# A fourth projection unit beside each head pair's RWKV preparation, two instead of three dealt out over the pair's groups

## What is computed

```python
h = rmsnorm(x, norm_g) * (1 + scale) + shift
proj = h @ w_in      # split into r, k, v, wd, ad, g, gq, gk, gv, ..., qd, kvd, kpe, ...
...
def step(s, inp):                       # per head, forward and backward in time
    sa = einsum('bhij,bhj->bhi', s, -kk_t)
    s = s * w_t + sa[..., None] * (kk_t * a_t) + v_t[..., None] * k_t
    return s, einsum('bhij,bhj->bhi', s, r_t)
...
o = groupnorm(outs[0] + outs[1]) + bonus
y_a = (o * silu(rw_g)) @ rw_out
```

## Time and profile before

| | us |
|---|---|
| median of 3 runs | 3240.06 |
| lowest and highest run | 3233.42, 3243.84 |
| the profiled execution | 3225.9 |
| its span, first to last instruction | 3224.1 |

### The profile page before, as it was taken

One profiled execution on the slowest core, in us unless ns is written; L12 is line 12 of the kernel. 1 busy time (PEld: TensorE's weight loads), 2 busy tenths in 40 slices (PEclk: granted clock), 3 DMA queues, 4 the chain that ended last, 5 costly groups with the idle time before them and its releaser, 6 DMA issues.

```text
span 3224.1 us, 70360 instructions
## 1 busy us (share of the span) xinstructions
PE 2882.2 (89%) x32136; PEld 1844.9 (57%) x32136; DVE 1178.7 (37%) x2271; ACT 859.3 (27%) x1510; POOL 29.9 (1%) x58
## 2 busy tenths in 40 slices
PE   8988888989787899999998888888888789999997
PEld 2565656565564556655556656565655555665554
DVE  2324243343647333311124243434255643341112
ACT  2323232332323333300013242323232424330000
POOL 0000000000000000000000000000000000000000
PEclk9999999999868799999999999998886769999999
DMA  7111010111000000112321000000010000002121
GB/s 289 47 42 42 23 61 23 49 35 43 33 7 30 14 14 20 74 66 71 96 79 35 18 22 24 22 23 23 16 35 14 20 17 21 14 22 72 66 76 66
DMA packets 35926, 142.32 MB, mean 44 GB/s; under 512 B 4592, under 2 KB 4624, under 8 KB 35120
## 3 DMA queue, kind: packets, MB, share of 16 engines
q1 hardware_dynamic: 31968, 116.68, 10.3%
q0 software_dynamic: 3664, 21.14, 1.9%
HBM read 130.82 MB, written 6.98 MB: 43 GB/s over the span
## 4 chain that ended last, share of the span: by engine, by line
PE 78%; DVE 10%; ACT 7%; issue 4%; DMA 0%; POOL 0%; DVEq 0%; ACTq 0%; SPq 0%
PE psum L509 74%; DVE tmp L1414 4%; PE psum L512 3%; DVE tmp L1411 2%; DVE tmp L1775 1%; DVE tmp L1422 1%; DVE tmp L1500 1%; ACT tmp L1159 1%; ACT acts L1159 0%; DMA ring<-units 0%; ACT L1154 0%; ACT tmp L1215 0%; DVE tmp L1714 0%; ACT tmp L1223 0%; ACT L1332 0%
## 5 line engine op out<-in xcount | busy, mean ns | idle before, releaser
L509 PE MATMUL psum<-hT,ring 128*128 128x128 f32 (+1 forms) x3904 | 1143.3, 446 | 13.5 <-DVE hT L1419 7.6
L509 PE MATMUL psum<-tmp 64*32 64x32 f32 (+8 forms) x8704 | 793.3, 293 | 154.0 <-DVE tmp L1414 76.7
L509 PEld LDWEIGHTS psum<-hT,ring 128*128 128x128 f32 x3904 | 622.0, 194 | 509.5 <-issue 496.1
L509 PEld LDWEIGHTS psum<-tmp 64*32 64x32 f32 (+5 forms) x8704 | 612.5, 170 | 324.4 <-issue 167.6
L509 PE MATMUL psum<-acts 32*32 32x32 f32 (+1 forms) x16080 | 221.1, 199 | 74.1 <-issue 53.6
L1159 ACT ACTIVATE acts<-psum 128x256 f32<-128x256 f32 (+5 forms) x230 | 108.1, 475 | 607.7 <-PE psum L509 607.6
L509 PEld LDWEIGHTS psum<-acts 32*32 32x32 f32 (+1 forms) x16080 | 190.3, 110 | 131.4 <-issue 99.4
L1159 ACT ACTIVATE tmp<-psum 128x256 f32<-128x256 f32 (+6 forms) x350 | 182.4, 527 | 261.5 <-PE psum L512 220.2
L509 PE MATMUL psum<-acts,ring 128*128 128x512 f32 (+1 forms) x768 | 210.8, 434 | 0.0
L509 PEld LDWEIGHTS psum<-acts,ring 128*128 128x128 f32 x768 | 117.3, 191 | 92.1 <-issue 92.1
L512 PE MATMUL psum<-con_sb,tmp 128*128 128x128 f32 x760 | 129.4, 299 | 42.4 <-DVE tmp L1414 35.5
(11 more groups left out here) (149 smaller groups left out, 1866.1 us busy)
## 6 DMA issues: line engine op xcount, KB each, us to landing
ring<-units SPq DMA_DIRECT2D x218, 512.0 KB, 3.2
small_sb<-small POOLq DMA_DIRECT2D x2, 3072.0 KB, 11.5
hT<-xT POOLq DMA_DIRECT2D x1, 2560.0 KB, 12.1
tmp<-xT POOLq DMA_DIRECT2D x8, 320.0 KB, 4.2
x_keep<-hT POOLq DMA_DIRECT2D x8, 320.0 KB, 4.4
tmp<-x_keep POOLq DMA_DIRECT2D x8, 320.0 KB, 3.3
yT<-acts POOLq DMA_DIRECT2D x8, 320.0 KB, 3.2
tmp<-masks SPq DMA_DIRECT2D x1, 1280.0 KB, 8.1
```

The lines of the kernel that those rows point to most:

```text
L509: return nc.tensor.matmul(out, lhsT, rhs, start=start, stop=stop, skip_group_check=True)
```

## The change

Each `BESIDE[p]` gets a fourth unit, taken from `BETWEEN[p]` of the same pair, which keeps two of three: k 2, v 3, gk 1 and qd 0 move. The second direction of the preparation now has two units behind its zw and za, on PE and on ACT. The order in which SP streams the units follows from the same lists. The number of units, of matmuls and of copies is the same as before. With 16 tiles instead of 24 over the same 38 beats, `beat_work` puts the tiles that remain into other beats.

```diff
-BESIDE = [[("k", 1), ("r", 1), ("v", 1)], [("v", 2), ("k", 3), ("r", 3)],
-          [("gq", 0), ("gq", 1), ("gk", 0)], [("gv", 1), ("gv", 2), ("gv", 3)]]
-BETWEEN = [[("g", 0), ("k", 2), ("r", 2)], [("g", 1), ("v", 3), ("misc", 0)], [("g", 2), ("gk", 1), ("gv", 0)],
-           [("g", 3), ("qd", 0), ("qd", 1)]]
+BESIDE = [[("k", 1), ("r", 1), ("v", 1), ("k", 2)], [("v", 2), ("k", 3), ("r", 3), ("v", 3)],
+          [("gq", 0), ("gq", 1), ("gk", 0), ("gk", 1)], [("gv", 1), ("gv", 2), ("gv", 3), ("qd", 0)]]
+BESIDE_AT = (slice(1, 2), slice(2, 4))
+BETWEEN = [[("g", 0), ("r", 2)], [("g", 1), ("misc", 0)], [("g", 2), ("gv", 0)], [("g", 3), ("qd", 1)]]
...
-                        for it in BESIDE[p][1 + d:2 + d]:
+                        for it in BESIDE[p][BESIDE_AT[d]]:
                             project(l, it)
```

## The result

The changed kernel takes 3269.28 us (median of 4 runs, 3261.36 to 3281.01) against 3236.74 us for the kernel before on the same chip (4 runs, 3227.13 to 3243.84): **1.0105 times as long, 95% interval 1.0061 to 1.0150**. It is slower by 33 us, where I had forecast 4 us less, and it lies outside the range.

What follows compares the result with a forecast made beforehand. PE was taken to bound the kernel, busy 2882 of 3224 us. Preparation +37.7, groups -40.0 and clock at XS -2.0 sum to -4.3 us, from the median 3240.06 to 3235.8; range 3213 to 3259.

Steps and rivals of the forecast that it cites:

- the groups' term, -40.0 us: Groups of all eight pairs: eight tiles fewer a pair give back 40.0 us of 71 us of PE work.
- beat 3: Groups, behind AV: the tile that leaves gives back 1.1 us, as T32's operands are there.
- my third rival: Groups: with fewer tiles PE stands more between small steps and the clock falls; slower, 3264, chance 0.14.
- The preparation, +37.7: End of the preparation: the fourth unit outlasts PE's wait for factors, so XS starts 37.7 us later in all.
- The clock at XS, -2: At XS, behind the preparation: without the gap the clock stays at 1.00, taken as 2 us saved in all.
- my 0.25: XS: the forecast's gain a pair from the full clock, in us.
- the bound of 2: XS: the most the full clock could save, 2 us a pair, 16 us in all.
- Both of my readings: XS to T16: instruction refill sets the pace (forecast), or it does not and the clock helps (rival, 3215, chance 0.22).
- The gate at beats 16 and 17, +1.7: Groups, behind AV: the gate unit's end delays Q64 by 1.7 us a pair in layer 1.
- The refill: Instruction fetch for PE: read as the pace of XS to T16; no term of its own in the sum.
- a rival of 0.09: Instruction stream: XS comes a quarter packet later, so lucky pairs can become unlucky; +19 us, 3254, chance 0.09.
- All tiles on PE's path: Groups: rival in which all 71 us of tiles come back; faster, 3205, chance 0.11.

Runs made afterwards that it cites:

- run 32: Not a follow-up run: the words say that the products that stayed take 32 us longer in the changed kernel's groups.
- e5: Kernel before, with two neighbouring 32x32 block products done as one, leaving out 7040 of 32136 matmul records: 3099.83 us.
- e6: Changed kernel with the same half of the block products left out: 3120.31 us.
- e9: e6 with five idle tiles, matmuls whose results nobody reads, in five of the beats: 3102.36 us.
- e13: Changed kernel with the PSUM bank turns of the idle tiles taken, but without their matmuls: 3278.21 us.
- e10: Changed kernel with five idle tiles, matmuls whose results nobody reads, in five of the beats: 3236.32 us.
- e1: Changed kernel with the gate unit second of the two, so that it ends at beat 35 instead of 16: 3274.55 us.
- e12: Changed kernel with its 16 tiles placed by hand and the gate's last tile in beat 21: 3230.55 us, 0.9996 of the kernel before.
- e3: Changed kernel with the old 24 tiles in the groups, a third unit there computing a copy nothing reads: 3272.55 us.

## Why the prediction was wrong

**The step that failed is the groups' term, -40.0 us.** It became +9. Its prices were right one by one, but for the gate's in layer 0 (below): beat 3 forecast at 1.1 and measured at 1.13, TF 0.1 and 0.1, Q128 0.7 and 0.7, Y 0.6 and 0.6, TaT 1.1 and 1.08, U 0.6 and 0.75 to 0.94, the tile that enters T16 0.5 and 0.6. What failed is the sum, which took PE's speed, and the waits for issue, as given. A tile in a beat does two things: it delays the next step, and it keeps PE at work while ACT or VectorE empties the last one. Without it PE stands for a bare wait at each step, the granted clock goes to 0.50, and the steps and tiles behind take nearly twice as long. That is my third rival, with a chance of 0.14 and a time of 3264; its mark, new stretches at 0.50 between T32 and the states, is what the trace shows (the two windows of pair 1 in the section on the result). I had priced it per stretch from rows 7, rightly, and took it for rare, because the trace of before had one such long stretch. It had 109 us at half clock in the groups already, which one view by windows would have told me.

The sums of the windows say how the +9 comes about. Eight tiles a pair less are 71 us of PE work at full clock, but PE is busy only 39.0 us less (846.4 after 885.4): the products that stayed run 32 us longer. PE stands still for 175.9 us instead of 127.9, 48 more, where 40 back out of 71 had allowed for 31; 23 of the 48 are waits for issue (72 before, 95 after), which I had put at nothing. So -71 + 32 + 48 = +9, and against the forecast the clock took 32 us and the issue waits 23, while the other waits came out 6 under it.

That the 32 us are the clock's is borne out by three more pairs of kernels, reckoned the same way: the work left over runs 18 us longer for 42 more at half clock (e5 to e6), 25 shorter for 65 fewer (e6 to e9), 42 shorter for 124 fewer (e13 to e10). With 32 for 91 here that is 0.34 to 0.43 us for each us at half clock. This is an estimate from one profile each.

**The preparation, +37.7.** Right in kind: XS comes late by what the unit is longer than the wait. XS starts 35.0 us later in sum, and it was 29.8 us to the end of XS. In pair 3 of layer 1 the two units take 17.50 us back to back instead of 17.84, so XS starts 4.1 us later and not 4.42, and XS then takes 1.95 us instead of 2.41.

**The clock at XS, -2.** The clock stays at 1.00 in XS, where it was 0.50 to 0.66, in seven pairs, and is 0.90 in one. In three pairs it falls behind XS, to 0.59 to 0.69, after an issue wait of 1.6 to 3.3 us in XS or just behind it. In pair 3 of layer 1 XS and the products up to the first 32x32 blocks take 3.78 us instead of 5.06, 1.3 us less. Over the eight pairs this stretch became 8.0 us shorter in sum, 1.0 a pair, between my 0.25 and the bound of 2; but the three pairs with these issue waits became 1.5 to 3.3 us longer. From XS to the end of T16, which takes in beat 1's tile too, 3.0 us of the gain are left. Both of my readings hold, each in some pairs.

**The gate at beats 16 and 17, +1.7.** Too small in layer 0. The timeline of pair 3 of layer 0 in the changed kernel, from the last tile:

```profile
755.63 1.30 PE L509 MATMUL psum<-hT,ring 128*128 128x512 f32 x4
...
756.23 1.28 ACT L1172 ACT_TABLE_LOAD   x1
...
757.53 0.70 ACT L1172 ACTIVATE acts<-psum 128x640 f32<-128x640 f32 x1
758.33 0.82 DVE L1414 TENSOR_TENSOR acts<-acts,psum 128x640 f32<-128x640 f32 x1 [4.93 <-ACT acts L1172]
...
759.30 1.63 PE L509 MATMUL psum<-acts 32*32 32x32 f32 x120 [2.37 <-DVE acts L1414]
...
764.66 0.33 PE L509 MATMUL psum<-acts 32*32 32x32 f32 x8 [3.73 <-issue]
```

The times of ACT and DVE are as forecast. But it is T32's own matmuls that wait, not only the addition behind them, and what they wait for is the product. By the kernel's order of banks I take it that the product sets free the PSUM banks of the gate unit, which are next in turn for T32. The wait of 2.37 us stands there in three of the four pairs of layer 0. In the same pair of the kernel before there was none:

```profile
737.53 1.29 PE L509 MATMUL psum<-acts 32*32 32x32 f32 x128
```

Then a wait for issue catches PE eight matmuls short of the end. With half of the blocks left out, where hardly a half clock or an issue wait is in it, T32 and Q64 cost 1.8 us a pair in layer 1, as forecast, and 9.6 us over layer 0, where I had 3.2. e1 moves this cost to beat 35 and gains nothing by it; e12, with the gate's end in beat 21, has no wait ahead of T32, but its tiles moved too.

**The refill.** I gave it +0 and a rival of 0.09. Issue waits rose by 19 us on the line of `mm`, by 23 inside the groups, and with half of the blocks left out the difference between the kernels fell by 12: it has a part. That these waits are the refill was only a reading so far; the trace bears it out for most. It also holds the times of the packets of the instruction queue (q8, rows 6). In the kernel before, 38 of the 46 issue waits of 0.8 us and more end 1.15 to 1.65 us behind the end of such a packet (62 of 84 us), but only 4 of the 90 other waits of PE of that length; in the changed kernel 46 of 54 (78 of 100 us). Why they became more stays open: e10 against e13 shows that tiles between the dense steps bring them down, not how. The alignment, which was the rival, is worth 5 to 10 us for the one shift tried, and moves both kernels alike. The rule of the Trainium skill (Runtime: NRT & Kernel Launch, section Instruction fetch mechanics) that the fetch hides behind dispatch disagrees with e5 too: PE's waits for issue fall from 98.4 to 38.5 us when blocks are left out.

**All tiles on PE's path.** e3 refutes this one: without 71 us of tiles the groups are 7 us shorter in sum, not 71.

## What to carry to other kernels

Work that fills the gaps of a chain of small products pays twice on this engine, as work and as what keeps its clock up; before taking it out, sum the time at half clock in the stretch, and look at whether the gaps left behind will lower it further. Move as much into a wait as the wait is long (here half a unit for 4.50 us, -15 us, with some tiles and the gate's end moved as well), not the next whole unit, whose surplus is paid in full. And do not let an item with a slow evacuation, a gate here, end ahead of a short step that takes its banks.

## What was not expected

- The clock falls without any long wait in these groups. In e6 a wait of 1.86 us, with shorter ones of 0.38 and 0.48 behind it, stands with a granted clock of 0.55 over 11.40 us.
- Work that nobody needs can shorten a kernel: 44 us of idle matmuls took 33 us off the changed kernel and did not make e6 slower (-18 us by the medians, -7 by the ratios), and in e9 all but 7 us of the half clock left the groups, which came down to 856.7 us.
- Leaving out 7040 small matmul records with their weight loads saved 137 us, some 20 ns each, 60 us of it in waits for issue, though the products that stayed have as many columns in sum: in these dense stretches it is the instructions, not the columns, that are paid for.
